# An expert stage that multiplies weights as they land: plain fp32 products in two column halves

## The reference

```python
def hier_moe(v, w_coarse, w_fine, w_gate, w_up, w_down):
    t = v.reshape(-1, D)
    ...                     # top-1 of 4 groups, then top-2 of 8 experts in it
    gates = jnp.sum(jax.nn.one_hot(eid, N_EXPERTS, dtype=jnp.float32) * wk[..., None], axis=1)
    hg = jnp.einsum('td,edf->tef', t, w_gate)
    hu = jnp.einsum('td,edf->tef', t, w_up)
    act = jax.nn.silu(hg) * hu * gates[:, :, None].astype(t.dtype)
    out = jnp.einsum('tef,efd->td', act, w_down)
    return out.reshape(bsz, L, D)
...
h = h + merged @ w_o
h = h + hier_moe(rmsnorm(h, norm2), w_coarse, w_fine, w_gate, w_up, w_down)
```

## Time and profile before

| | |
|---|---|
| median of three runs | 1604.57 us (1603.33 to 1604.58) |
| profiled execution | 1605.18 us |
| its span, first to last instruction | 1603.4 us |
| PE busy | 1482.1 us, 92% |
| DVE, ACT busy | 994.9 and 859.2 us |
| mean DMA rate over the span | 214 GB/s |

### The profile page before, as it was taken

One profiled execution on the slowest core, in us unless ns is written; L12 is line 12 of the kernel. 1 busy time (PEld: TensorE's weight loads), 2 busy tenths in 40 slices (PEclk: granted clock), 3 DMA queues, 4 the chain that ended last, 5 costly groups with the idle time before them and its releaser, 6 DMA issues.

```text
span 1603.4 us, 21338 instructions
## 1 busy us (share of the span) xinstructions
PE 1482.1 (92%) x7946; PEld 1295.8 (81%) x7946; DVE 994.9 (62%) x1253; ACT 859.2 (54%) x1073; POOL 166.2 (10%) x169
## 2 busy tenths in 40 slices
PE   3999999999999999999999996899999999999960
PEld 2999999999999999999999996676666666666630
DVE  5495777887773344332342225888887887877826
ACT  5465455565553233222242224688878778778732
POOL 0000000000000000000000001121322223222102
PEclk9999999999999999999999997899999999999985
DMA  9233433223333445444343364799999999999925
GB/s 238 61 120 115 124 102 103 90 82 115 119 108 110 127 139 196 127 130 131 123 139 115 125 224 174 267 395 393 401 396 403 400 395 403 395 383 398 392 85 226
DMA packets 160179, 343.49 MB, mean 214 GB/s; under 512 B 25446, under 2 KB 132134, under 8 KB 132200
## 3 DMA queue, kind: packets, MB, share of 16 engines
q1 hardware_dynamic: 149216, 324.82, 57.0%
q0 software_dynamic: 5632, 16.02, 3.0%
q10 hardware_dynamic: 5272, 1.84, 0.5%
HBM read 340.03 MB, written 23.58 MB: 227 GB/s over the span
## 4 chain that ended last, share of the span: by engine, by line
PE 68%; DMA 17%; DVE 8%; ACT 5%; issue 3%; ACTq 0%; SPq 0%; DVEq 0%; POOL 0%; POOLq 0%
PE PS L1047 49%; DMA mraw_b<-w_down 6%; PE PS L1278 6%; PE PS L1304 4%; DMA mraw_d<-w_down 4%; DMA mraw_a<-w_down 4%; DVE mLg L1828 2%; PE PS L1299 2%; ACT mHg L886 2%; DMA mraw_b<-w_up 1%; PE PS L1266 1%; PE PS L1099 1%; DVE spL L1371 1%; PE PS L1072 1%; DMA yk<-ybuf 1%
## 5 line engine op out<-in xcount | busy, mean ns | idle before, releaser
L1047 PE MATMUL PS<-uHL,spH 128*128 128x384 f32 (+2 forms) x2560 | 665.3, 341 | 3.1 <-DVE uHL L1489 1.4
L1047 PEld LDWEIGHTS PS<-uHL,spH 128*128 128x128 f32 x2560 | 464.6, 188 | 4.7 <-issue 2.5
L1371 DVE TENSOR_TENSOR spL<-raw,spH 128x2048 fp32r<-128x2048 f32 x100 | 229.0, 2291 | 340.3 <-ACT spH L633 339.1
L1047 PE MATMUL PS<-uHL,spL 128*128 128x384 f32 (+2 forms) x1280 | 433.5, 339 | 0.0
L633 ACT ACTIVATE spH<-raw 128x2048 fp32r<-128x2048 f32 x100 | 191.2, 1913 | 312.0 <-PE PS L1047 311.7
L1047 PEld LDWEIGHTS PS<-uHL,spL 128*128 128x128 f32 x1280 | 242.0, 189 | 0.0
L1278 PE MATMUL PS<-mHg,xS 128*128 128x512 f32 x512 | 207.4, 405 | 4.1 <-issue 3.9
L1278 PE MATMUL PS<-mLg,xS 128*128 128x512 f32 x512 | 203.9, 398 | 0.0
L1828 DVE TENSOR_TENSOR mLg<-mraw_b,mHg 128x2048 fp32r<-128x2048 f32 x53 | 119.7, 2289 | 35.8 <-ACT mHg L886 35.8
L1047 PE MATMUL PS<-tHL,spH 128*128 128x384 f32 x512 | 130.3, 335 | 0.0
L1278 PEld LDWEIGHTS PS<-mHg,xS 128*128 128x128 f32 x512 | 99.4, 194 | 26.9 <-issue 4.0
(11 more groups left out here) (349 smaller groups left out, 1873.2 us busy)
## 6 DMA issues: line engine op xcount, KB each, us to landing
raw<-w_in SPq DMA_DIRECT2D x64, 1024.0 KB, 5.8
mraw_b<-w_gate SPq DMA_DIRECT2D x31, 1024.0 KB
mraw_b<-w_down SPq DMA_DIRECT2D x31, 1024.0 KB
mraw_a<-w_down SPq DMA_DIRECT2D x23, 1024.0 KB
mraw_a<-w_gate SPq DMA_DIRECT2D x22, 1024.0 KB
mraw_b<-w_up SPq DMA_DIRECT2D x22, 1024.0 KB
mraw_a<-w_up SPq DMA_DIRECT2D x21, 1024.0 KB
raw<-w_o SPq DMA_DIRECT2D x16, 1024.0 KB, 5.6
```

Source lines behind the costliest of these rows:

```text
L1047: ins = pe.matmul(PS[:, b + m, 0:w_], PT[w][:, s, k * UW + m * P:k * UW + (m + 1) * P], rhs[:, a, k0 + k, c0:], start=first and k == 0 and ...
L1371: dve.tensor_tensor(spL[:, s, :], raw[:, s, :], spH[:, s, :].bitcast(F32), ALU.subtract).then_inc(lo_done, 1)
```

## The change

The experts' weights are no longer split. `xS` holds the 64 token columns once, in fp32, and `gate_up` multiplies them with the landed unit itself, in plain fp32. Gate and up are two products of 256 columns: gate's result goes to output rows 0 to 63, up's to rows 64 to 127 (index `g`), which are two halves of the array's columns; both use all 128 rows. `down` does the same with the two halves of its 2048 output columns and needs two PSUM banks where it had four. The functions `low`, `gs`, `mhi_`, `mlo_`, `al` and the zero columns beside `aTH`, `aTL`, `aTF` go. ACT copies the first eight blocks of the transposed rows, DVE the others; of y, ACT copies the left half and DVE the right (`y_left`, `y_right`). The product for the gate weights runs twice (L1249 before), so that they stand in rows 0 to 63 and 64 to 127.

In the space of the split parts there are now three sets of six landing buffers. SyncE's list asks for a set's units as soon as the products that read them three experts ago are done. The overflow path and all that is ahead of the router stay.

```diff
-MRAW = 9
-NAT = 1
+SETS = 3
...
+        u_off = {0: [a_m, a_m + UB, a_m + 2 * UB, a_h + Q * D * 4, a_k + 1152 + KD * 2 * C * 4, a_h + UB],
+                 1: [x * UB for x in range(6)],
+                 2: [8 * UB, 9 * UB, 10 * UB, 11 * UB, a_h + 2 * UB, 6 * UB]}
+        mun = [[at(f"mun{x}_{n}", o, [P, UNIT]) for n, o in enumerate(u_off[x])] for x in range(SETS)]
+        mgu = [[m[0:2], m[2:4]] for m in mun]
+        mdn = [m[4:6] for m in mun]
...
-            def mload(u, i, src, k):
-                old = u - MRAW
-                if old >= 0 and SPLIT[old]:
-                    sp.wait_ge(mlo, split_to(old, i) + (old < 8 and not isinstance(i, int)))
-                elif old >= 0:
-                    sp.wait_ge(dn_done, PER * i + UNITS[old][1] + 1)
-                sp.dma_start(mraw[u % MRAW].rearrange("p (k c) -> p k c", k=k), src).then_inc(m_in[u % MRAW], 16)
...
+            def load_gu(e, c, half, n=2):
+                x = c % SETS
+                for m, w in zip(mgu[x][half][0:n], (w_gate_v, w_up_v)):
+                    sp.dma_start(m.rearrange("p (k c) -> p k c", k=UK),
+                                 w[e][:, half * UK:(half + 1) * UK, :]).then_inc(gu_in[x][half], 16)
+            def load_d(e, c, k):
+                sp.dma_start(mdn[c % SETS][k].rearrange("p (k c) -> p k c", k=1),
+                             w_down_v[e][:, k:k + 1, :]).then_inc(dn_in[c % SETS], 16)
+            def load_e(e, c):
+                sp.wait_ge(gu_half, e - (SETS - 1))
+                load_gu(e, c, 0)
+                sp.wait_ge(gu_full, e - (SETS - 1))
+                load_gu(e, c, 1)
+                ge(sp, dn_done, e - SETS)
+                if c == SETS:
+                    sp.wait_ge(rt_done, 1)
+                for k in range(2):
+                    load_d(e - 1, c - 1, k)
             sp.wait_ge(ml_done, 4)
...
+            load_gu(0, 0, 0)
+            load_gu(0, 0, 1)
+            load_d(0, 0, 0)
             for g in range(ND2 - 3, ND2):
                 v_store(g)
             sp.wait_ge(htr, ND2)
-            mload(5, 0, w_up_v[1][:, 0:UK, :], UK)
-            load_gu(1, 1, 0, 1)
-            mload(8, 0, w_down_v[0][:, 0:1, :], 1)
...
+            load_gu(1, 1, 0)
+            load_gu(1, 1, 1)
+            sp.wait_ge(v_out, 16 * ND2)
+            load_d(0, 0, 1)
+            load_gu(2, 2, 0)
+            load_gu(2, 2, 1)
+            for k in range(2):
+                load_d(1, 1, k)
+            load_e(SETS, SETS)
+            with sp.Fori(0, (NE - SETS - 1) // PER) as i:
+                for j in range(SETS + 1, SETS + 1 + PER):
+                    load_e(PER * i + j, j)
+            for e in range(SETS + 1 + (NE - SETS - 1) // PER * PER, NE):
+                load_e(e, e)
+            sp.wait_ge(dn_done, NE - SETS)
+            for k in range(2):
+                load_d(NE - 1, NE - 1, k)
...
-            def mhi_(u, i, s, free=None):
-                act.wait_ge(m_in[u % MRAW], landed(u, i))
-                if free is not None:
-                    ge(act, *free)
-                act.activation(mH[s], mraw[u % MRAW], ACT.Copy).then_inc(mhi, 1)
...
-            def low(e):
-                act.wait_ge(gu_full, e + 1)
-                ge(act, am_done, e)
-                act.activation(gu[0:C, :], PS[XM:XM + C, 0, :], ACT.Copy).then_inc(low_done, 1)
+            def xh(e):
+                act.wait_ge(xg_tr, e * 2 + 1)
+                act.activation(xS[:, 0:8, :], PS[:, 2, :].rearrange("p (k c) -> p k c", k=8),
+                               ACT.Copy).then_inc(xh_done, 1)
...
-            def y_out(e):
+                act.activation(aTF[:, :, :], PS[:, 1, 0:2 * P].rearrange("p (k c) -> p k c", k=2)[:, :, C:],
+                               ACT.Copy).then_inc(ah_done, 1)
+            def y_left(e):
                 act.wait_ge(dn_done, e + 1)
                 ge(act, yo_out, e * 16)
-                act.activation(yo[0:C, :].rearrange("p (n c) -> p n c", n=4), PS[0:C, 4:8, :],
+                act.activation(yo[0:C, 0:D // 2].rearrange("p (n c) -> p n c", n=2), PS[0:C, 4:6, :],
                                ACT.Copy).then_inc(yo_done, 1)
             def silu(e):
-                act.wait_ge(gs_done, e + 1)
-                act.activation(sg[0:C, :], gu[0:C, 0:DE], ACT.Silu,
+                act.wait_ge(gu_full, e + 1)
+                ge(act, am_done, e)
+                act.activation(sg[C:2 * C, :], PS[0:C, 0, 0:DE], ACT.Silu,
                                scale=rslots[0:C, bass.ds(e, 1)]).then_inc(silu_done, 1)
...
+            def body(e, c):
                 if c > 0:
                     ah(e - 1)
-                    if c == 1:
-                        act.wait_ge(v_out, 16 * ND2)
-                    for k in range(2 - NAT):
-                        mhi_(dn_unit(c - 1, k), i, 4 + k, (dn_done, e - 1))
-                if c > 1:
-                    y_out(e - 2)
-                if c < NE - 1:
-                    for h in range(2):
-                        mhi_(gu_unit(c + 1) + h, i, h, (gu_half, e + 1))
-                low(e)
-                if c < NE - 1:
-                    xh(e + 1, 0)
+                if c == 0:
+                    act.wait_ge(slp_done, 2)
+                    act.wait_ge(rs_done2, 1)
                 silu(e)
                 if c < NE - 1:
-                    xh(e + 1, 1)
-                    for h in range(2):
-                        mhi_(gu_unit(c + 1) + 2 + h, i, 2 + h, None)
+                    xh(e + 1)
+                if c == 1:
+                    act.wait_ge(v_out, 16 * ND2)
+                if c > 0:
+                    y_left(e - 1)
...
                 for half in range(2):
-                    pe.wait_ge(mlo, split_to(gu_unit(c) + 2 * half + 1, i))
+                    pe.wait_ge(gu_in[c % SETS][half], landed(c, i))
                     for k in range(UK):
-                        for w in range(2):
-                            ins = pe.matmul(PS[:, 0, 0:2 * DE], xS[:, half * UK + k, :],
-                                            MG[w][:, 2 * half:2 * half + 2, k * DE:(k + 1) * DE],
-                                            start=half == 0 and k == 0 and w == 0,
-                                            stop=half == 1 and k == UK - 1 and w == 1)
+                        for g in range(2):
+                            ins = pe.matmul(PS[C * g:C * (g + 1), 0, 0:DE], xS[:, half * UK + k, :],
+                                            mgu[c % SETS][half][g][:, k * DE:(k + 1) * DE],
+                                            start=half == 0 and k == 0, stop=half == 1 and k == UK - 1)
                     ins.then_inc(gu_full if half else gu_half, 1)
...
             def down(e, c, i):
-                pe.wait_ge(al_done, e + 1)
+                pe.wait_ge(ah_done, e + 1)
                 ge(pe, yo_done, e)
-                pe.wait_ge(mlo, split_to(dn_unit(c, 0), i))
-                for x in range(4):
-                    for w, a in PASSES:
-                        pe.matmul(PS[0:CM, 4 + x, :], AT[a][:, :], MD[w][:, 0, x * 512:(x + 1) * 512],
-                                  start=(w, a) == (0, 0), stop=False)
-                r = (dn_unit(c, 1)) % MRAW
-                pe.wait_ge(m_in[r], landed(dn_unit(c, 1), i))
-                for x in range(4):
-                    ins = pe.matmul(PS[0:CM, 4 + x, :], aTF[:, :], mraw[r][:, x * 512:(x + 1) * 512],
-                                    start=False, stop=True)
+                ge(pe, yr_done, e)
+                pe.wait_ge(dn_in[c % SETS], landed(c, i))
+                for k in range(2):
+                    for x in range(2):
+                        for g in range(2):
+                            ins = pe.matmul(PS[C * g:C * (g + 1), 4 + x, :], aTF[:, k, :],
+                                            mdn[c % SETS][k][:, (2 * g + x) * 512:(2 * g + x + 1) * 512],
+                                            start=k == 0, stop=k == 1)
                 ins.then_inc(dn_done, 1)
...
-            def mlo_(u, i, s):
-                dve.wait_ge(mhi, split_to(u, i))
-                TT(mL[s], mraw[u % MRAW], mH[s].bitcast(F32), ALU.subtract).then_inc(mlo, 1)
...
-            def gs(e):
-                dve.wait_ge(low_done, e + 1)
-                TT(gu[0:C, :], PS[0:C, 0, :], gu[0:C, :], ALU.add).then_inc(gs_done, 1)
-            def al(e):
-                dve.wait_ge(ah_done, e + 1)
-                TT(aTL[:, 0:C], PS[:, 1, 0:C], aTH[:, 0:C].bitcast(F32), ALU.subtract).then_inc(al_done, 1)
+            dve.tensor_copy(rslots[:, :], PS[:, 1, 0:NE]).then_inc(rs_done2, 1)
+            def xl(e):
+                dve.wait_ge(xg_tr, e * 2 + 2)
+                dve.tensor_copy(xS[:, 8:16, :], PS[:, 3, :].rearrange("p (k c) -> p k c", k=8)).then_inc(xl_done, 1)
...
+            def y_right(e):
+                dve.wait_ge(dn_done, e + 1)
+                ge(dve, yo_out, e * 16)
+                dve.tensor_copy(yo[0:C, D // 2:].rearrange("p (n c) -> p n c", n=2),
```

(10 more changed lines are left out.)

184 lines of the change are left out of this document (47 added, 137 removed).

## The result

The changed kernel takes **1577.47 us** (median of four runs, 1577.1 to 1578.11) against 1603.95 for the kernel before: a ratio of 0.983, 95% interval 0.9818 to 0.9842. That is 26.5 us less; 39.8 were forecast (1565 us, range 1554 to 1584). The profiled execution took 1577.5, its span is 1575.8.

What follows compares the result with a forecast made beforehand. Reading weights by DMA was taken to bound most of the expert stage. Loads end at 1510, y out 6.1 us later, plus 47.5: span 1563.6, 39.8 less than before; 1604.57 - 39.8 = 1565 us, range 1554 to 1584.

Steps and rivals of the forecast that it cites:

- Products: PE work per expert in plain fp32 on two column halves: 12.8 to 15.5 us, 13 taken.
- serial price: PE time per expert if the two column halves run one after the other: 23.1 us.
- Rival (a): Column halves do not run side by side, PE sets the pace at 23.1 us per expert; about 1795 us, chance 0.08.
- Rival (b): PE's weight loads do not hide behind products: 23.9 us per expert, about 1820 us; chance 0.03.
- Rival (c): The one xg buffer becomes the bound if gathers land late, from 12.8 us; at 15.4, about 1645 us; chance 0.05.
- Rival (d): PE cools while waiting and its clock halves; two such stretches per expert put the end at about 1590; chance 0.03.
- The start: Loads after the router: queue fed until 1012 to 1014 us, no gap, or up to 8 us if the gather is late.
- The loads: Expert stage: 208.0 MB at 397 GB/s take 524 us from 985, ending at 1510 with a start-up microsecond.
- The sign that was named: In the trace after, DMA share near 1 from 986 to about 1510 us with no hole.
- From the last load to y: End of the stage: y out 6.1 us after the last load, at 1516.1, between 4.7 and 9.
- what follows y: From y out to the end of the span: 47.5 us, which the change does not touch.
- The range: 1554 to 1584 us, the forecast's own, holding about 8 in 10.

Runs made afterwards that it cites:

- e7_tail: Changed kernel with nothing of expert 31 waiting for 30 and act's transposes of 31 moved ahead of down of 30; 1576.4 us, ratio 0.9826.
- e11_pairs_even: Changed kernel with token slots laid out for dealing in pairs and ranks shifted by twice the expert's number in its group; 1569.45 us, ratio 0.9778.
- e14_half_rows: Changed kernel with each token row gathered as two 4 KB half rows into 128 partitions instead of one 8 KB row into 64; 1546.5 us, ratio 0.9637.
- e4_rows_even: Changed kernel with every rank shifted by twice the expert's number in its group, slots otherwise as they were; 1580.32 us, ratio 0.9848.

## Why the prediction was right, and where it was off

**Products: right.** 13.41 us per expert, 13 taken; the serial price of 23.1 measured 23.74. PE's waits for landed weights are 67.0 us, in mid stage some 2.4 per expert where 3 to 4 were forecast. Rival (a) is excluded by the pair 7.06 and 13.96.

**Rival (b): excluded.** In the changed kernel a weight load lasts 142 ns in the mean, which would be 9.1 us for 64 loads if they stood alone; the 64 products with all their loads take 7.06. The Trainium skill's rule (TensorE: Matmul & The Clock Gate, Part 3, "What overlaps and what doesn't") does not hold here: loads overlap though both halves use the same rows.

```profile
L1226 PEld LDWEIGHTS PS<-mun,xS 128*64 128x64 f32 x1792 | 132.0, 142 | 142.7 <-DMA mun<-w_up 76.8 <-issue 13.2
```

**Rival (c): excluded.** Weights land 25 to 30 us after their issue now, so many stand in the queue, and a gather still lands in 7.7 us in the median, as in the earlier trace rows; PE waits for none in mid stage. (From 1040 to 1500 us, changed kernel:)

```profile
xg<-vbuf,idg POOLq DMA_INDIRECT x28, 7.7
```

**Rival (d): it happens, hidden in mid stage and not quite at the end.** The granted clock is 0.97 in mid stage, where the loads set the pace. At the end PE waits for w_down of 30 and the clock falls to half; down of 30 takes 5.37 us where it takes 3.65 in `e7_tail`. That is part of the 2 us which `e7_tail` saves behind the last landing.

**The start: right.** No hole, 385 GB/s; the third set of buffers carries 10.5 us of the gain.

**The loads: the step that failed.** "At 397 that is 524 us; from 985 it ends at 1509" took the queue for one pipe. The mean was right: with even rows the queue is full until 1510 and empty by 1514 (`e11_pairs_even`). But 16 engines end each in its own time, and a unit has landed only when the last of them has. In the changed kernel the last unit lands at 1519.9 and not at 1510; with even rows it is 1512.3. This one term is 9.9 us of the 12.2 by which the span was missed. The sign that was named, a share near 1 to about 1510, failed at 1502.

The trace of before showed it. "Loads arrive until 1526 us" is a misreading: there too the share falls from 1522 on, and bytes still move after 1530 (columns as in the earlier trace rows), but the splits and PE behind them hid that.

```profile
1522.00:1523.00 1.00, 1.00 (x5) 1.00 0.71 295
...
1530.00:1531.00 1.00, 1.00 (x6) 1.00 0.20 82
```

**From the last load to y: near in size.** 6.1 us forecast; 7.2 in the changed kernel (1519.9 to 1527.06), 5.6 with even rows, 5.1 in `e7_tail`. The order was wrong: down of 30 was to end 2 us before the last landing and ended 0.5 behind it, at 1520.42, since its own w_down came late and the clock was at half. This is 1.1 of the 12.2 us. The other 1.2 are in what follows y, 48.7 against 47.5.

**The range: held, partly by luck.** Its upper end stood for a slower mean rate, a hole at the start and half clock at the end. Of these only the half clock came; the lag of single engines, which made most of the difference, had no term in it.

**A term taken for a constant.** 397 GB/s was read as what the engines can move. It is 420 to 422 less the dip of every gather: 422 without gathers, 420 with gathers spread over 128 partitions. Both kernels paid for it, so it cost the forecast nothing, but it was the larger gain: 31 us with `e14_half_rows`.

## What to carry over

When loads set the end, ask when the last DMA engine ends, not when the bytes are moved at the mean rate; a share that sinks while loads are outstanding is the sign, and here it told of unequal work beside the loads. A DMA share of 1 is no proof that the engines move what they can: compare the GB/s of short stretches at the same share. Where plain fp32 products have few output rows, two column halves halved their time here, and the space of the split parts went to buffers that keep the queue filled.

## What was not expected of the hardware

- A gather of some 24 rows of 8 KB into 64 partitions lowers all traffic from 421 to 330 GB/s for about 3 us; scatters from 64 partitions leave it at 418, and a gather into 128 partitions at 417.
- Where the used rows of a 64-row indirect transfer stand moves the last landing of 208 MB of loads: 1523.7 in `e4_rows_even`, 1519.9 in the changed kernel, 1512.3 in `e11_pairs_even`. That the rows are dealt to the engines in pairs fits these runs and is not shown directly.
- Plain fp32 products on two column halves ran 1.98 times as fast as one after the other, 0.99 of two, where the four groups of the earlier trace rows had 0.79 of four.
